# Ten slots for experts' weights instead of six, slot-number columns copied by VectorE, and LayerNorm shifts on ScalarE

## The reference, cut to what matters

```python
h = modulate(layer_norm(x + gate * mixer(h)))      # deepnorm, x is scaled by ALPHA
s = sigmoid(h @ router)                            # 64 experts, 8 groups
w, idx = top-6 experts of the 4 best groups        # weights, 6 experts for each token
y  = silu(h @ sh_gate) * (h @ sh_up) @ sh_down     # shared expert
y += sum over the 6 experts e: w_e * (silu(h @ gate_e) * (h @ up_e)) @ down_e
x = layer_norm(ALPHA * x + g * y)
```

## Time and profile before

| | us |
|---|---|
| median of three runs (2867.58 to 2873.2) | 2872.71 |
| the profiled execution | 2876.89 |
| span of its profile, first to last instruction | 2875.6 |
| mean granted TensorE clock, share of 2.4 GHz | 0.981 |
| pairs of the first mixture of experts | 1443.9 to 1975 |
| pairs of the second | 2294.4 to 2845 |

### The profile page before, as it was taken

The page is one execution under the profiler, slowest core; times in us unless marked ns, Lnnn a source line. Parts: engine busy times, 40 slices in busy tenths (PEclk is TensorE's granted clock), DMA queues, the critical chain, the costliest instruction groups (busy, mean ns, idle before and its releaser), DMA issues.

```text
span 2875.6 us, 42230 instructions
## 1 busy us (share of the span) xinstructions
PE 2714.1 (94%) x16738; PEld 1944.7 (68%) x16738; DVE 1048.9 (36%) x2342; ACT 484.2 (17%) x1056; POOL 103.0 (4%) x98
## 2 busy tenths in 40 slices
PE   7998899999998999999899999998999899999997
PEld 5776678887776888878755555555888655555554
DVE  3455323324465234233352222223663362222223
ACT  2322301002232210012111111111332111111111
POOL 0000000000000000000010000000000010000000
PEclk9999999999999999999999999999999999999999
DMA  5222246663232367655189999995323199999995
GB/s 198 74 103 99 89 164 234 256 237 120 88 105 101 118 233 272 240 201 205 62 337 395 399 398 401 401 401 215 127 80 133 55 407 393 404 397 381 399 393 208
DMA packets 104990, 684.56 MB, mean 238 GB/s; under 512 B 17761, under 2 KB 19313, under 8 KB 24497
## 3 DMA queue, kind: packets, MB, share of 16 engines
q1 hardware_dynamic: 93040, 665.02, 59.2%
q0 software_dynamic: 11264, 16.54, 1.7%
q10 hardware_dynamic: 576, 1.43, 0.1%
HBM read 703.37 MB, written 4.19 MB: 246 GB/s over the span
## 4 chain that ended last, share of the span: by engine, by line
PE 79%; DMA 12%; DVE 5%; ACT 2%; issue 1%; SPq 0%; ACTq 0%; DVEq 0%
PE PS L483 75%; DMA wmoe<-in_experts 12%; PE PS L488 4%; ACT AR L2279 1%; ACT AR L2329 1%; DMA COLS<-in_cols 0%; SPq L2900 0%; DVE ST L1418 0%; DVE AR L1415 0%; ACT ST L2279 0%; DVE X L1694 0%; DVE AR L1587 0%; ACT wmoe L2279 0%; DVE AR L1585 0%; DVE AR L1426 0%
## 5 line engine op out<-in xcount | busy, mean ns | idle before, releaser
L483 PE MATMUL PS<-wmoe,AR 128*64 128x256 f32 (+2 forms) x5488 | 723.1, 419 | 40.8 <-DMA wmoe<-in_experts 28.2
L483 PE MATMUL PS<-H,wdense 128*128 128x256 f32 (+1 forms) x3056 | 706.7, 391 | 9.3 <-DVE H L1450 3.6
L483 PEld LDWEIGHTS PS<-H,wdense 128*128 128x128 f32 x3056 | 583.8, 193 | 115.6 <-issue 11.6
L483 PEld LDWEIGHTS PS<-wmoe,AR 128*64 128x64 f32 (+1 forms) x5488 | 389.1, 137 | 327.7 <-issue 148.2
L2279 ACT ACTIVATE AR<-PS 128x256 f32<-128x256 f32 (+7 forms) x515 | 228.6, 451 | 1553.8 <-PE PS L483 946.0
L483 PE MATMUL PS<-AR,wdense 128*128 128x256 f32 (+1 forms) x1920 | 434.1, 387 | 7.1 <-DVE AR L1637 2.9
L483 PEld LDWEIGHTS PS<-AR,wdense 128*128 128x128 f32 x1920 | 366.5, 191 | 71.0 <-issue 3.7
L483 PE MATMUL PS<-AR 128*128 128x512 f32 (+17 forms) x1604 | 370.0, 393 | 30.4 <-DVE AR L1426 12.9
L483 PEld LDWEIGHTS PS<-AR 128*128 128x128 f32 (+6 forms) x1604 | 189.1, 183 | 121.0 <-issue 84.2
L488 PEld LDWEIGHTS PS<-CST,AR 128*128 128x128 f32 (+4 forms) x1118 | 127.5, 135 | 152.6 <-issue 131.6
L488 PE MATMUL PS<-CST,AR 128*128 128x128 f32 (+4 forms) x1118 | 179.8, 276 | 6.0 <-DVE AR L2233 3.2
(11 more groups left out here) (275 smaller groups left out, 1271.4 us busy)
## 6 DMA issues: line engine op xcount, KB each, us to landing
wmoe<-in_experts SPq DMA_DIRECT2D x402, 1024.0 KB, 8.9
wdense<-in_dense SPq DMA_DIRECT2D x176, 1024.0 KB, 4.8
wmoe<-in_ada SPq DMA_DIRECT2D x48, 1024.0 KB, 7.0
tokens<-AR POOLq DMA_DIRECT2D x4, 512.0 KB, 2.9
wdense<-in_dense SPq DMA_DIRECT2D x2, 768.0 KB, 10.3
wdense<-in_dense SPq DMA_DIRECT2D x2, 640.0 KB, 6.2
CST<-in_const SPq DMA_DIRECT2D x1, 1197.0 KB, 19.0
AR<-tokens,IX POOLq DMA_INDIRECT x71, 7.8
```

Of the source, the lines that this page charges most:

```text
L483: return te.matmul(out, lhsT, rhs, start=start, stop=stop, skip_group_check=True)
```

## The change

- **Ten slots.** The gate and up matrices of even pairs go to slots 0 to 3 of `wmoe`, those of odd pairs to the four slots of the dense ring, and the down matrices of every pair to slots 4 and 5 of `wmoe`. The gate and up matrices of pair 1 are loaded before pair 0, each as soon as the dense matrix in its slot has been used; the two down matrices of pair 0 are loaded before it too.
- **Order of transfers.** In `turn` for pair p, the gate and up matrices now wait for `gu` of pair p-2 (they waited for pair p-1), the down matrices of pair p-1 still for `d 1` of pair p-1. In "more", all turns use the dense slots, so there the wait is for the pair before, as it was. The last two down matrices go to slots 0 and 1.
- **Loops.** `STATIC` is 7 and the loop "pairs" has 12 turns of two pairs each on every engine but GpSimd.
- **Slot numbers.** `choose` first copies the three columns of the pair to a fixed place `M_WC` (one more VectorE instruction for each pair), and TensorE's `numbers` reads from there.
- **LayerNorm.** VectorE multiplies the 8 chunks by `ST` in a row, ScalarE does gain and shift of each chunk (`Identity` with scale and bias columns). `scaled_and_shifted` on VectorE waits for ScalarE's chunk.

```diff
-STATIC = 6
+STATIC = 7
+    def gate_slot(u, j, at):
+        return WD[:, (at + j) % dense.depth] if u else WM[:, j]
...
-            def numbers(p, *label):
+            def numbers(*label):
                 for t in range(2):
-                    m = mm(PS[:, B_D[1], 0:3], M_PM[:, t], M_WA[:, t, bass.ds(p, 1), :], start=t == 0, stop=t == 1)
+                    m = mm(PS[:, B_D[1], 0:3], M_PM[:, t], M_WC[:, t, :], start=t == 0, stop=t == 1)
...
-            with repeat(te, PE, NE // 2 - 1 - STATIC, "pairs", L) as i:
-                pair(("pairs", L), i + STATIC, landed_in(n0, i), 16 * (STATIC + 2) + 16 * i, True,
+            with repeat(te, PE, (NE // 2 - 1 - STATIC) // 2, "pairs", L) as i:
+                for u in range(2):
+                    p = STATIC + u
+                    pair(("pairs", L, u), i * 2 + p, gates(p % 2, 16 * (p // 2 + 1) + 16 * i), downs(16 * p + 32 * i),
...
             ve.wait_ge(AC.sem, AC.of(what, "scale"))
-            for c in range(DC + 1):
-                if c < DC:
-                    VE.up(ve.tensor_tensor(X2[:, c, :], X2[:, c, :], ST[:, 0:S], ALU.mult))
-                if c > 0:
-                    ve.wait_ge(VE.sem, VE.so_far() - (c < DC))
-                    finish(c - 1)
+            for c in range(DC):
+                VE.up(ve.tensor_tensor(X2[:, c, :], X2[:, c, :], ST[:, 0:S], ALU.mult), what, "normed", c)
...
             def choose(p, *label):
+                VE.up(ve.tensor_copy(M_WC, M_WA[:, :, bass.ds(p, 1), :].rearrange("p t o w -> p t (o w)")))
...
+            for c in range(DC):
+                ac.wait_ge(VE.sem, VE.of(what, "normed", c))
+                AC.up(act(dst[:, c, :], X2[:, c, :], ACT.Identity, shift(c), gain(c)), *label, c)
...
             e = [weights(L, j) for j in range(4)]
-            for n, src in enumerate((e[0][0], e[1][0], e[0][1], e[1][1], e[2][0], e[3][0])):
-                fill(n, src)
+            for j in range(4):
+                fill_gates(0, j, e[j % 2][j // 2])
+            for j in range(2):
+                fill_down(j, e[j][2])
             load(count)
-            used(("pair", L, 0, "gu", 0))
-            fill(6, e[2][1])
-            fill(7, e[3][1])
-            used(("pair", L, 0, "gu", 1))
-            fill(8, e[0][2])
-            fill(9, e[1][2])
+            for j in range(4):
+                epoch, use = dense_at.get(loads[0] - 4 + j, (0, 1))
+                sp.wait_ge(PES[epoch].sem, use)
+                fill_gates(1, j, e[2 + j % 2][j // 2])
...
+            def turn(u, of, gates_used, downs_used):
+                for g in range(2):
+                    gates_used(g)
+                    for q in range(2):
+                        fill_gates(u, 2 * g + q, of(g, q))
+                downs_used()
+                for q in range(2):
+                    fill_down(q, of(2, q))
...
-            sp.wait_ge(PE.sem, PE.of("more", L, "gu", 0) - per + per * turns)
             for q in range(2):
-                sp.dma_start(WM[:, 4 + q],
+                sp.dma_start(WM[:, q],
                              weights_at(L, entry(turns * 2 + q))[2]).then_inc(tails[L][q], 16)
+            sp.wait_ge(PE.sem, PE.of("more", L, "gu", 1) - per + per * turns)
```

More of the change, by code:

```diff
@@ L1199, in gate_up @@
                 for g in range(2):
-                    w = [slots(2 * g + e, DC, 256) for e in range(2)]
+                    w = [slots(2 * g + e).rearrange("p (k w) -> p k w", k=DC) for e in range(2)]
                     for k in range(DC):
@@ L1207, in down @@
             def down(slots, what):
-                w = [slots(e, 2, D) for e in range(2)]
+                w = [slots(e).rearrange("p (k w) -> p k w", k=2) for e in range(2)]
                 for q in range(2):
@@ L1224, in turn_hidden, with gates, slot, downs @@
                 PE.up(m, *what)
[L1226 to L1239, removed]
+            def gates(u, count):
+                def slot(j):
+                    te.wait_ge(gates_landed[L][u][j], count)
+                    return gate_slot(u, j, free)
+                return slot
+            def downs(count):
+                def slot(j):
+                    te.wait_ge(downs_landed[L][j], count)
+                    return WM[:, 4 + j]
+                return slot
+            def pair(what, p, gates, downs, landings, before, at):
                 PE.at[what + ("added before",)] = PE.n - 1
                 te.wait_ge(AC.sem, at(AC, what + ("x1 read before",)))
-                gate_up(lambda j, k, w: slots(j, k, w), what + ("gu",))
+                gate_up(gates, what + ("gu",))
                 if before:
@@ L1248, in pair @@
                     te.wait_ge(VE.sem, at(VE, what + ("numbers before",)))
-                    down(lambda j, k, w: slots(4 + j, k, w), what + ("d",))
+                    down(downs, what + ("d",))
                 te.wait_ge(tokens_landed[L], landings)
@@ L1259, in pair @@
                     te.wait_ge(VE.sem, at(VE, what + ("ye", 1)))
-                numbers(p + 2, *what, "numbers")
+                numbers(*what, "numbers")
                 if before:
@@ L2214, in moe_layer @@
             own()
-            with repeat(ve, VE, NE // 2 - 1 - STATIC, "pairs", L) as i:
-                pair(("pairs", L), i + STATIC, True, lambda done, label: done.of(*label) + done.turns_of("pairs", L) * i)
+            with repeat(ve, VE, (NE // 2 - 1 - STATIC) // 2, "pairs", L) as i:
+                for u in range(2):
+                    pair(("pairs", L, u), i * 2 + (STATIC + u), True, lambda done, label: done.of(*label) + done.turns_of("pairs", L) * i)
             VE.mark("before more", L)
@@ L2481, in first_layer, with layer_norm @@
                         AC.up(act(SQX[:, bass.ds(i * 4 + 2 * u, 2), :], X[:, bass.ds(i * 4 + 2 * u, 2), :], Square), "ff2 squared", L, u)
-        def layer_norm(what):
+        def layer_norm(what, dst, gain, shift, *label):
             for c in range(DC):
@@ L2736, in moe_layer @@
                 pair(("pair", L, p), static)
-            with repeat(ac, AC, NE // 2 - 1 - STATIC, "pairs", L) as i:
-                pair(("pairs", L), lambda done, label: done.of(*label) + done.turns_of("pairs", L) * i)
+            with repeat(ac, AC, (NE // 2 - 1 - STATIC) // 2, "pairs", L) as i:
+                for u in range(2):
+                    pair(("pairs", L, u), lambda done, label: done.of(*label) + done.turns_of("pairs", L) * i)
             AC.mark("before more", L)
```

105 lines of the change are left out of this document (51 added, 54 removed).

## The result

The changed kernel takes 2833.27 us (median of 4 runs, 2828.53 to 2836.52), the kernel before 2871.28 us (4 runs, 2867.58 to 2873.2): a ratio of 0.9867, with a 95% interval of 0.9853 to 0.9882, or 38.0 us faster. I had forecast 2855, 17.4 us faster, with 2836 as the lower end. The result is rival (B), in which TensorE becomes the bound of the pairs. The profiled execution of the changed kernel took 2834.15 us with a span of 2832.8.

The account below looks back on a forecast made before the run. The DMA was taken to pace the pairs, TensorE being 0.7 us a pair faster. Slots 14.0, LayerNorm 3.4 and routers 0.3, less 0.3 for slot numbers, made 17.4 us: 2872.71 to 2855.3 us, range 2836 to 2869.

Parts of the forecast that it names:

- rival (B): Pairs: deeper queue raises the rate or the cushion does all it can, TensorE becomes the bound; 24 to 49 us faster, chance 0.15.
- The floor: Pairs: TensorE's own length of a pair without waits, 15.62 us.
- SyncE's order, its gap behind pair 0 and its bursts: SyncE's queue: fills in bursts of six at each `d 1`, the DMA idle some 6.3 us after the first fills.
- The net head start: Ahead of pair 0: four transfers moved earlier, 10.5 us, less 6.3 us of DMA idling; 4.2 us gained for each layer.
- (D): Loop of pairs: doubled body makes jumps back wait for instructions; slower, 2918 us, chance 0.06 (0.11 with other ways to be slower).
- More slots bring no bandwidth: Pairs: slots only move transfers ahead of pair 0 and fill the 2% idle DMA; the rate stays at 398 GB/s.
- a quarter of the idle time, 2.8 us: Pairs: share of 10.5 us idle DMA time taken as returning in each layer; bounds 0 and 17 or 20 us.
- the cushion: Pairs: supply delay absorbed before TensorE waits for down matrices, some 5 us in the new order against 1.8 us before.
- LayerNorm: Last chunk 1.7 us earlier at `odd h` and at the output, 3.4 us together; ScalarE taken at 0.41 us a chunk.
- my 0.15 us each: Routers: LayerNorm's first chunk reaches TensorE earlier, 2 x 0.15 = 0.3 us faster.
- The slot numbers: `choose`: the copy costs 0.15 us where TensorE waits for VectorE's first choice, 0.3 us slower in all.

Follow-up runs that it names:

- lean_before: Kernel before with half of the k steps of the gate and up products left out, output not the reference's; 2866.69 us, ratio 0.9982.
- even_flow_12: even_flow with two more slots, so each pair's down matrices are issued a pair earlier, without bursts of six; 2829.23 us, ratio 0.9852.
- loops_copies: Kernel before with only loops of two pairs and the copied slot numbers, six slots in their old order; 2873.76 us, ratio 1.001.
- the shallow kernels: Four kernels whose transfers land as early as in the kernel before; mean distances from pair 1 to the last pair 500.2 and 517.3 us.
- norm_only: Kernel before with the LayerNorm part of the change alone; 2866.45 us, ratio 0.9983.
- even_flow: Changed kernel with down matrices issued a pair later, at `d 1` behind four other fills, instead of bursts of six; 2867.63 us, ratio 0.9988.

## Why the prediction was wrong

**What held.** That the supply of weights sets the pace of the pairs before, and that TensorE could go 0.7 us a pair faster: lean_before shows it, since half the work in `gate_up` gives only 4 us. The floor held, 15.62 us a pair: 31 of them are 484.2 us, and even_flow_12 has 484.2. SyncE's order, its gap behind pair 0 and its bursts were as described. The net head start was taken as 4.2 us a layer, and its removal costs 3.0 and 3.3 in single executions. Twice as long loops cost nothing (loops_copies), against (D); over 1560 to 1880, ten turns of the new loop, the changed kernel's instruction queue moved a single packet:

```profile
q8 instruction: 1, 0.02, 0.0%
```

The Trainium skill ("Runtime: NRT & Kernel Launch", Instruction fetch mechanics) has a taken branch out of two held lines force a fetch; this row shows one packet at most for the ten jumps back in its stretch, so they fetched no block each.

**The step that failed** is the sentence "More slots bring no bandwidth", and behind it the term "a quarter of the idle time, 2.8 us" (a quarter of 10.5 us is 2.6 us; the slip is small beside the miss). I read a DMA share of 0.98 as an engine that is full, and 398 GB/s as what it can give, so that I let more slots return only the head start and a part of the 2%. The runs show 412 to 417 GB/s where more transfers stand in the queue, while the share goes only from 0.99 to 1.01: 2% to 3% in the share, 3% to 4% in the rate, and the share's scale does not end at 1.00. In its low windows the kernel before moved a quarter less than in the others while the share fell only to 0.91, so the share hid most of what was missing. The term measured 15.2 us in the first layer and 19.6 in the second (19.4 and 23.8 less the 4.2), or about 10 and 13 against the usual distances of the shallow kernels. With the head start that is nearly all of the waits that there were, 21.4 and 24.4. My argument against (B), that the 404 GB/s window already had a share of 1.00, was the wrong way round. That window and the 420 to 428 of the better slices showed that the engines could give more than 398 at nearly the same share. The mean was low because of one short stretch in every pair, around `gu 0`, when the queue ran low. Slices of a few microseconds show it, and I had rested the argument on means over hundreds of microseconds. The Trainium skill's 435 GB/s ("DMA: Bandwidth & Descriptors", Specifications), which I had set aside, pointed to (B), and 417 sustained lies under it. Its 358 GB/s as HBM's limit for one core is exceeded in every kernel here.

I had also put the cushion in numbers (5 us to lose where it was 1.8) and then given it a quarter. Since TensorE needed only 4% more than the supply gave, the gain was capped at the waits, and a supply improved by 4% takes all of them. The sum had bounds of 0 and all of the waits, and nothing in the rows spoke for a quarter.

**LayerNorm** was the right mechanism, oversized. I took 0.41 us a chunk on ScalarE.

```profile
1980.51 2.77 DVE L1703 TENSOR_TENSOR X<-X,ST 128x256 f32<-128x256 f32 x8 [2.96 <-ACT ST L2279]
1980.97 4.04 ACT L2279 ACTIVATE H<-X,AFF 128x256 f32<-128x256 f32 x8 [0.49 <-DVE X L1703]
1981.71 7.37 PE L491 MATMUL PS<-wdense,H 128*128 128x16 f32 x32 [2.20 <-DVE X L1703]
...
2825.94 2.77 DVE L1703 TENSOR_TENSOR X<-X,ST 128x256 f32<-128x256 f32 x8 [2.96 <-ACT ST L2279]
2826.40 4.04 ACT L2279 ACTIVATE X<-X,COLS 128x256 f32<-128x256 f32 x8 [0.49 <-DVE X L1703]
2827.56 3.28 SPq L2981 DMA_DIRECT2D out_xT<-X  x4
```

Eight shifts take 4.04 us, 0.505 each. The last chunk is done 1980.97 + 4.04 - 1980.51 = 4.50 us after VectorE's start, where it was 5.52: 1.0 us earlier and not 1.7. This comes back in both places. At `odd h`, TensorE's products end 8.57 us after VectorE's start, where they ended 9.56 us after it; at the output, the span ends 6.86 us after it, where it ended 7.86 us after it. norm_only has the same 8.57 and 6.85. That makes 2.0 us in place of 3.4. norm_only's gain of 4.7 us has an interval of 1.1 to 8.3 us and settles no more than the sign.

At the routers my 0.15 us each can't be told, because the granted clock moves more. The first router's 32 products (the window 1403.50 to 1410 stands above):

```profile
1403.49 6.78 PE L491 MATMUL PS<-RTR,H 128*128 128x64 f32 x32 [2.20 <-DVE X L1703]
```

**The slot numbers** cost no more than was forecast: the copy takes 0.16 us, and TensorE's wait for the first choice grew only from 3.68 to 3.74.

```profile
1431.90 0.16 DVE L2118 COPY AR<-AR 128x6 f32<-128x6 f32 x1
...
1432.54 0.99 PE L491 MATMUL PS<-AR 128*128 128x3 f32 x4 [3.74 <-DVE AR L2119]
```

**What stays open** is what happens inside the 16 DMA engines when the queue runs low. That the rate that the kernel before loses lies in short stretches, about one in each pair, and that it goes with how early the fills are issued and not with their place, the bursts or TensorE's pace, is shown. Why the busy share stays at 1.01 in a window that moves 272 GB/s is not; the gathers have only 0.8% of it. The runs varied how early slots may be filled, never how one transfer is cut, and that wasn't tried.

## What to carry to other kernels

A DMA share of 0.98 is not the proof that the DMA can give no more: look at the rate in slices of half a period and shorter. Here the best slices of 8 us were 7% above the mean, and the low ones came once a period, where SyncE had issued nothing for 8 us. Count what is under way by dividing the time to landing by the time of one transfer, and free slots early enough that transfers remain in the queue up to the next issue; an average of five or six did it here. More slots that wait for each other in one queue's order do not help, as even_flow shows. Where two resources are within a few per cent of each other, the gain of a better supply ends where the other resource becomes the bound; here it was nearly the whole of the waits, so don't put it at a fraction of them unless a row gives that fraction.

## What was unexpected of the hardware

The mean rate of one core's weight transfers of 1 MB goes with how many are under way on average: 396 to 405 GB/s with about three and a half, 409 and 411 with four, 412 to 414 with about five, 417 with six. It is a matter of gaps: the median of 2 us windows is 418 GB/s with the short queue and with the long one, and the short queue adds about one window of some 300 GB/s in each pair. The busy share of the DMA engines in these low windows was 0.91, and 1.01 in one of them, so it says little of what they move.

ScalarE's shift with a scale and a bias column takes 0.505 us for 128x256, back to back, against 0.34 for the squares of the same size.

The router's same 32 products took 6.78 us at a granted clock of 0.52, 6.02 us at 0.76 in the kernel before, and 4.01 us at 1.00, in even_flow_12:

```profile
1402.36 4.01 PE L492 MATMUL PS<-RTR,H 128*128 128x64 f32 x32 [2.20 <-DVE X L1704]
...
1402.40:1406.20 3.80, 3.80 (x32) 3.80 (x33) 3.76 (x12) 3.78 (x8) 0.00 (x0) 1.00 0.00 0
```

TensorE had been idle for 2.20 us ahead of it in the slowest and in the fastest of these alike, and the granted clock was 1.00 up to this gap in both. The clock was near its lower level of 1.2 GHz in the one and at its upper of 2.4 GHz in the other, and the 2.8 us between them are more than what the change does to the router. I did not find out what decides it.
